# One tile is normed, scored and routed beside the output product, and the slabs behind it are paced by four slots

## The reference, cut to what matters

```python
h = h + einsum('btc,cd->btd', mixed, w_out)                # the output product
xb = rmsnorm(h, ffn_norm_w)                                # for each block of 128 tokens:
q = einsum('nd,dc->nc', xb, w_query).reshape(128, 8, 2, 128)
s = einsum('nhpc,hpkc->nhpk', q, subkeys)                  # 8 heads, 2 halves, 128 keys
sv, si = top_k(s, 16)
cand_s = sv[:, :, 0, :, None] + sv[:, :, 1, None, :]       # 16 x 16 candidates
cand_i = si[:, :, 0, :, None] * 128 + si[:, :, 1, None, :]
top_s, pos = top_k(cand_s.flat, 16)                        # 16 experts of a head
experts, gates = cand_i[pos], softmax(top_s)               # 128 experts of a token
hid = gelu(einsum('nkd,nd->nk', u_table[experts], xb)) * gates
y = einsum('nk,nkd->nd', hid, v_table[experts])
```

## Time and profile before

| what | value |
|---|---|
| median of 3 runs | 2848.63 us (2845.56 to 2849.38) |
| profiled execution, its own time | 2850.17 us |
| its span, first to last instruction | 2848.4 us |
| its mean granted TensorE clock | 0.978 |
| PE, DVE, ACT, POOL busy | 91%, 65%, 45%, 25% of the span |
| HBM read | 746.77 MB, 263 GB/s over the span |

### The profile page before, as it was taken

One profiled execution on the slowest core, in us unless ns is written; L12 is line 12 of the kernel. 1 busy time (PEld: TensorE's weight loads), 2 busy tenths in 40 slices (PEclk: granted clock), 3 DMA queues, 4 the chain that ended last, 5 costly groups with the idle time before them and its releaser, 6 DMA issues. The chain is left out here.

```text
span 2848.4 us, 32530 instructions
## 1 busy us (share of the span) xinstructions
PE 2594.6 (91%) x11450; PEld 1789.5 (63%) x11450; DVE 1840.9 (65%) x3807; ACT 1282.7 (45%) x2860; POOL 707.6 (25%) x661
## 2 busy tenths in 40 slices
PE   8998969989799977799989999899999898999998
PEld 8886755434355523255555555399788577788887
DVE  7787467777777767777777776655564774433323
ACT  3244234454454445556556555445325564232222
POOL 3210014444344434444444434200000110000000
PEclk9999989999899999999999999999999999999999
DMA  7853049999999999999999999766332103132322
GB/s 286 280 162 122 16 184 406 421 410 407 394 420 420 416 415 418 416 413 419 419 412 410 417 415 415 289 193 209 106 96 58 39 24 111 45 103 90 104 96 74
DMA packets 133843, 751.11 MB, mean 264 GB/s; under 512 B 19504, under 2 KB 20048, under 8 KB 67472
## 3 DMA queue, kind: packets, MB, share of 16 engines
q0 software_dynamic: 82320, 575.94, 50.0%
q1 hardware_dynamic: 51072, 173.02, 17.4%
q10 hardware_dynamic: 288, 0.07, 0.0%
HBM read 746.77 MB, written 2.10 MB: 263 GB/s over the span
## 5 line engine op out<-in xcount | busy, mean ns | idle before, releaser
L1848 PE MATMUL peer_y<-rows,diag 128*128 128x512 f32 x2048 | 996.3, 613 | 152.4 <-ACT diag L1828 141.0
L1802 DVE CUSTOM_DVE_ANT_0 rows<-rows,hidden 128x1024 f32<-128x1024 f32 x512 | 627.4, 1225 | 353.0 <-DMA rows<-in_peer_table,experts 350.7
L1789 POOL DMA_INDIRECT rows<-in_peer_table,experts x512 | 608.0, 1187 | 952.3 <-PE peer_y L1848 793.4
L1848 PEld LDWEIGHTS peer_y<-rows,diag 128*128 128x128 f32 x2048 | 364.0, 192 | 549.7 <-issue 293.2
L1825 ACT ACTIVATE hid<-hid 128x1 f32<-128x1 f32 x512 | 102.6, 200 | 530.0 <-DVE hid L1802 526.4
L2462 DVE TENSOR_TENSOR piece_w_low<-piece_raw,piece_w_high 128x1024 fp32r<-128x1024 f32 x132 | 161.4, 1223 | 96.7 <-ACT piece_w_high L2457 96.5
L1828 ACT ACTIVATE diag<-ident,hid 128x128 f32<-128x128 f32 x512 | 205.6, 401 | 16.6
L2457 ACT ACTIVATE piece_w_high<-piece_raw 128x1024 fp32r<-128x1024 f32 x132 | 138.8, 1052 | 105.0 <-PE out_bank L161 77.6
L1826 ACT ACTIVATE hid<-hid,gates 128x1 f32<-128x1 f32 x512 | 150.8, 295 | 16.6
L159 PE MATMUL peer_y<-peer_feat_high,early_w_high 128*128 128x256 f32 x352 | 144.5, 410 | 1.8 <-issue 1.8
L426 ACT ACTIVATE proj_w_high<-proj_raw 128x1024 fp32r<-128x1024 f32 (+2 forms) x57 | 57.6, 1013 | 189.5 <-PE proj_pair L161 98.9
(11 more groups left out here) (624 smaller groups left out, 5541.5 us busy)
## 6 DMA issues: line engine op xcount, KB each, us to landing
ada<-in_w_ada POOLq DMA_DIRECT2D x96, 384.0 KB, 4.6
piece_raw<-in_ffn_w_gate SPq DMA_DIRECT2D x44, 512.0 KB, 3.5
piece_raw<-in_ffn_w_up SPq DMA_DIRECT2D x44, 512.0 KB, 4.4
piece_raw<-in_ffn_w_down SPq DMA_DIRECT2D x44, 512.0 KB, 3.5
query_raw<-in_peer_w_query SPq DMA_DIRECT2D x32, 512.0 KB, 7.9
early_raw<-in_ffn_w_gate SPq DMA_DIRECT2D x22, 512.0 KB, 8.2
early_raw<-in_ffn_w_up SPq DMA_DIRECT2D x22, 512.0 KB, 8.0
early_raw<-in_ffn_w_down SPq DMA_DIRECT2D x22, 512.0 KB, 7.8
```

The source lines that it names most:

```text
L1789: pool.indirect_dma_start(self.rows[:, b, :], None, self.table, bass.IndirectOffsetOnAxis(ap=self.experts[:, unit % self.SETS, n % TOPK:n ...
L1802: dve.tensor_tensor_reduce(out=self.rows[:, b, 0:D], in0=self.rows[:, b, 0:D], in1=self.hidden[:, tile, :], scale=1.0, scalar=0.0, op0=ALU ...
L1848: last = pe.matmul(self.y[self.bank(tile)][:, c * BANK:(c + 1) * BANK], self.diag[:, b, :], self.rows[:, b, D + c * BANK:D + (c + 1) * BAN ...
```

## The change

Tile 0 is normed alone, as soon as its two units of the output product are added, in the first half of unit 2 of the product. Its features, two slabs of queries with 128 columns only (`first_query`), their scores (against keys loaded beforehand in a small tile of their own) and 14 routing steps of unit 0 run in the block of the output product, before unit 3's sum is added and tile 1 is normed. POOL gathers slots 0 to 3 in that block, and slots 4 and 5 when tile 1's features are done, since the scratch tiles of the norm now lie in those two buffers. The slabs' first two are split earlier. The 24 `column` products of units 0 to 3 all stand in units 0 and 1. In `peer_scores` slabs 0 and 1 are asked for tile 1 only; AHEAD is 4 and PACE 4 in the first half, so that slabs 4 to 15 have slots beside them, and END is 56, not 58. The load of all keys moves from the end of the output product to the head of that block. Behind the first six dots no routing step is done, behind the next 16 two, then one. The exponentials of a unit are done on ACT ahead of the slot's work at other slots than before (`exps_before`).

```diff
...
+    FREE_ROWS, ROUTED = 4, 14
...
-        behind = Scratch(nc, t.meta_at + 4 * D, None)
-        tile_sq = behind.sbuf("peer_sq", [P, 2, D])
+        last_rows = experts.last_rows(FREE_ROWS)
+        tile_sq = last_rows.sbuf("peer_sq", [P, D])
         tile_ss = spare.sbuf("peer_ss", [P, 2])
-        diag = behind.sbuf("peer_diag", [P, 2, P])
-        full = behind.sbuf("peer_full", [P, 2, 2, W2])
+        diag = last_rows.sbuf("peer_diag", [P, 2, P])
+        full = last_rows.sbuf("peer_full", [P, 2, 4, P])
+        first_keys = last_rows.sbuf("first_keys", [P, 2, NK])
...
+        peer_bank = [l_bank[1], l_bank[2]]
+        first_q = [l_bank[3][:, 0, :], l_bank[1][:, 0, :]]
+        first_s = l_bank[2][:, 0:2, :]
...
-            sp.wait_ge(out_done, 4)
-            sp.dma_start(keys[:, :, :], dram["peer_subkeys"]).then_inc(keys_in.handle, 16)
+            sp.wait_ge(o_summed, TT)
+            sp.dma_start(first_keys[:, :, :], dram["peer_subkeys"][:, 0:2, :]).then_inc(keys_in.handle, 16)
+            experts.load(sp, dram)
...
+            experts.gathers_to(pool, FREE_ROWS)
+            pool.wait_ge(low, 4)
+            experts.gathers_to(pool, experts.RING)
...
             weights.high_first(act)
...
+            def tile_root(i):
+                act.wait_ge(x_added, 2 * i + 2)
+                act.activation(tile_sq[:, :], t.x[:, i, :], ACT.Square, accum_out=tile_ss[:, i:i + 1]).then_inc(tile_summed, 1)
+                act.wait_ge(tile_ms, i + 1)
+                act.activation(tile_ss[:, i:i + 1], tile_ss[:, i:i + 1], ACT.Sqrt).then_inc(tile_rstd, 1)
+            def tile_high(i):
+                for g in range(2):
+                    act.wait_ge(whole, 2 * i + g + 1)
+                    act.activation(feat_parts.high[:, 4 * g:4 * g + 4, i * P:(i + 1) * P], full[:, g, :, :], ACT.Copy)\
+                       .then_inc(high, 1)
+            tile_root(0)
+            tile_high(0)
+            for b in range(2):
+                act.wait_ge(weights.used.handle, weights.used.at(b + 1))
+                act.activation(query[:, b, 0:P], first_q[b], ACT.Copy).then_inc(first_moved, 1)
+            act.wait_ge(tile_rstd, 1)
+            tile_root(1)
+            tile_high(1)
+            experts.exponentials(act, 0)
...
-            for u in range(4):
+            dve.wait_ge(turned, 4)
+            weights.low_first(dve)
+            def add_rows(u):
                 tile, c = u // 2, u % 2
                 dve.wait_ge(out_done, u + 1)
                 x = t.x[:, tile, c * BANK:(c + 1) * BANK]
                 dve.tensor_tensor(x, x, turn_bank[u], ALU.add).then_inc(x_added, 1)
...
+            def tile_scale(i):
+                own = tile_ss[:, i:i + 1]
+                dve.wait_ge(tile_summed, i + 1)
+                chain.link(dve.tensor_scalar(own, own, 1.0 / D, EPS, ALU.mult, ALU.add))
+                dve.reciprocal(own, own).then_inc(tile_ms, 1)
+                dve.wait_ge(tile_rstd, i + 1)
+                dve.tensor_scalar(diag[:, i, :], t.ident[:, :], own, None, ALU.mult).then_inc(diag_ready, 1)
+            def tile_parts(i):
+                for g in range(2):
+                    dve.wait_ge(bank_turned, 2 * i + g + 1)
+                    if i:
+                        dve.wait_ge(low, g + 1)
+                    for f in range(4 * g, 4 * g + 4):
+                        last = dve.tensor_scalar(full[:, g, f % 4, :], peer_bank[g][:, f % 4, :], t.ffn_norm[:, f:f + 1], None,
+                                                 ALU.mult)
+                    last.then_inc(whole, 1)
+                for g in range(2):
+                    own = (slice(0, P), slice(4 * g, 4 * g + 4), slice(i * P, (i + 1) * P))
+                    dve.wait_ge(high, 2 * i + g + 1)
+                    dve.tensor_tensor(feat_parts.low[own], full[:, g, :, :], feat_parts.high[own].bitcast(F32), ALU.subtract)\
+                       .then_inc(low, 1)
+            def tile_hidden(i):
+                dve.scalar_tensor_tensor(hidden[:, i, :], t.x[:, i, :], tile_ss[:, i:i + 1], row_w[:, :], ALU.mult, ALU.mult)
+            add_rows(0)
+            add_rows(1)
+            tile_scale(0)
+            add_rows(2)
+            tile_parts(0)
             dve.wait_ge(row_in, 16)
-            for i in range(2):
-                dve.scalar_tensor_tensor(hidden[:, i, :], t.x[:, i, :], tile_ss[:, i:i + 1], row_w[:, :], ALU.mult, ALU.mult)
-            weights.low_first(dve)
-            for g in range(5):
-                if g < 4:
-                    dve.wait_ge(bank_turned, g + 1)
-                    if g >= 2:
-                        dve.wait_ge(low, g - 1)
-                    for f in (2 * g, 2 * g + 1):
-                        last = dve.tensor_scalar(full[:, g % 2, f % 2, :], peer_bank[g][:, f % 2, :], t.ffn_norm[:, f:f + 1],
-                                                 None, ALU.mult)
-                    last.then_inc(whole, 1)
-                if g >= 1:
-                    two = slice(2 * g - 2, 2 * g)
-                    dve.wait_ge(high, g)
-                    dve.tensor_tensor(feat_parts.low[:, two, :], full[:, (g - 1) % 2, :, :],
-                                      feat_parts.high[:, two, :].bitcast(F32), ALU.subtract).then_inc(low, 1)
+            tile_hidden(0)
+            dve.wait_ge(first_scored, 2)
+            chain.link(dve.tensor_copy(scores[:, 0:2, :], first_s))
+            experts.route(dve, ROUTED)
+            add_rows(3)
+            tile_scale(1)
+            tile_parts(1)
+            tile_hidden(1)
...
-            for u in range(4):
+            def out_rows(u, chunks):
                 i, c = u // 2, u % 2
-                for f in range(KC):
+                for f in chunks:
                     last = pe.matmul(turn_bank[u], feat[:, f, i * P:(i + 1) * P], w_out[:, c, f, :],
                                      start=(f == 0), stop=(f == KC - 1))
-                    if f % 4 < 3:
-                        column(24 + 6 * u + f // 4 * 3 + f % 4)
-                last.then_inc(out_done, 1)
-            pe.wait_ge(diag_ready, 1)
-            for g in range(4):
-                for f in (2 * g, 2 * g + 1):
-                    for i in range(2):
-                        last = pe.matmul(peer_bank[g][:, f % 2, i * P:(i + 1) * P], t.x[:, i, f * P:(f + 1) * P], diag[:, i, :],
-                                         start=True, stop=True)
-                last.then_inc(bank_turned, 1)
+                    if u < 2 and f % 4 < 3:
+                        for n in range(2):
+                            column(24 + 12 * u + f // 4 * 6 + f % 4 * 2 + n)
+                    if f == KC - 1:
+                        last.then_inc(out_done, 1)
+            def turn_tile(i):
+                pe.wait_ge(diag_ready, i + 1)
+                for f in range(KC):
+                    last = pe.matmul(peer_bank[f // 4][:, f % 4, :], t.x[:, i, f * P:(f + 1) * P], diag[:, i, :], start=True,
+                                     stop=True)
+                    if f % 4 == 3:
+                        last.then_inc(bank_turned, 1)
+            def first_query(b):
+                pe.wait_ge(weights.low.handle, weights.low.at(b + 1))
+                for k in range(KC):
+                    last = product(pe, first_q[b], weights.columns(b, slice(k * P, (k + 1) * P)),
+                                   (feat_parts.high[:, k, 0:P], feat_parts.low[:, k, 0:P]), start=(k == 0), stop=(k == KC - 1))
+                last.then_inc(weights.used.handle, 1)
+            def first_score(b):
+                pe.wait_ge(first_moved, b + 1)
+                pe.matmul(first_s[:, b, :], query[:, b, 0:P], first_keys[:, b, :], start=True, stop=True)\
+                    .then_inc(first_scored, 1)
+            out_rows(0, range(KC))
+            out_rows(1, range(KC))
+            out_rows(2, range(4))
+            turn_tile(0)
+            out_rows(2, range(4, KC))
+            pe.wait_ge(low, 2)
+            first_query(0)
+            first_query(1)
+            out_rows(3, range(1))
+            pe.wait_ge(keys_in.handle, keys_in.at(16))
+            first_score(0)
+            first_score(1)
+            out_rows(3, range(1, KC))
+            turn_tile(1)
...
+    QB, RING, PACE = 2 * PH, weights.RING, 5 if half else 4
+    AHEAD = 0 if half else 4
...
+        def tiles_of(b):
+            return range(int(half == 0 and b < 2), 2)
+        def columns_of(b):
+            return slice(tiles_of(b).start * P, W)
...
-                experts.load(sp, dram)
+                sp.dma_start(keys[:, :, :], dram["peer_subkeys"]).then_inc(keys_in.handle, 16)
...
+                own = columns_of(b)
...
-                if half == 0 and b == max(ROUTE) + 1:
-                    experts.exponentials(act, 0)
...
-                if half == 0 and b in ROUTE:
-                    if b == min(ROUTE):
-                        dve.wait_ge(s_moved.handle, s_moved.at(2))
-                    experts.route(dve, ROUTE[b])
...
+    STEPS, BEHIND = TOPK, 6
```

(49 more changed lines are left out.)

28 lines of the change are left out of this document (9 added, 19 removed).

## The result

| | before | after |
|---|---|---|
| median | 2849.06 us (5 runs, 2845.56 to 2850.09) | 2864.38 us (5 runs, 2862.28 to 2866.68) |
| profiled span | 2848.4 us | 2863.1 us |
| granted clock, mean of the span | 0.978 | 0.976 |

The account below looks back on a forecast made before the run. Bytes bound the gather stretch, so the start of continuous transfer sets the end. Full flow 4.6 us later, less 0.2 for fewer bytes, gave +4.4 on the median 2848.63: 2853.0 us, range 2844 to 2864.

Parts of the forecast that it names:

- Part 2: Tile 0's features after unit 2 of the output product: PE waits uncovered from 359.6 to 364.5, 4.9 us.
- Part 3: Tile 0's two 128-column slabs: 5.4 us for the first, 2.9 for the second; routing begins at 374.5.
- Part 4: Routing and first gathers: first gather asked at 383.7, 16.6 us earlier than before; next block starts at 395.2.
- Part 5: Block of scores to first dot: slab 2 lands 8.6 us in, first dot at 414.9, 2 us later than before.
- the 81 ns quoted in Part 3: Skill's figure for a 128-column load and product: a slab would be 1.9 us, the total some 3 us better; not adopted.
- The sum itself: Slot 0 free at 422.6, full flow at 424.6: 4.6 us later, less 0.2 for 0.1 MB, makes +4.4 us.
- rival (c): Gather stretch from 460 on runs at 418 GB/s, not 414, as requests come steadier: net -8.6, 2840 us; chance 0.11.
- (b): DVE or PE becomes the bound in the 48 slots, a slab taking 12.0 instead of 11.4 us: 2860 us; chance 0.08.
- Rival (a): Half-wide products in slabs 0 and 1 of both tiles cost like f32 ones: +13.6 in all, 2862 us; chance 0.21.
- Rival (d): High clock throughout and slab 2 landing as if alone: net -2.2, 2846.4 us; chance 0.10.

Follow-up runs that it names:

- e2: Changed kernel with slabs 2 and 3 and the full keys asked in the earlier block, that of the output product; 2858.87 us, ratio 1.0036.
- e4: Changed kernel with no gather in the block of the output product, the ring of six asked in the block of scores; 2863.71 us, ratio 1.0058.
- e1: Changed kernel with all eight chunks of unit 3 of the output product ahead of tile 0's two half-wide slabs; 2861.85 us, ratio 1.0045.
- e3: e2 with slabs 0 and 1 of the block of scores multiplied for both tiles, 256 columns; 2853.35 us, ratio 1.0019.
- e7: Kernel before with only the new pace (AHEAD 4, PACE 4, END 56, routing steps and exponentials moved), merge block as before; 2847.54 us, ratio 0.9996.
- e12: Kernel before with the new pace of e7 and the early split of e8, merge block untouched; 2842.60 us, ratio 0.9978.
- e5: Changed kernel with the edits of e1, e2 and e3 together, full keys asked when the first scores are made; 2849.99 us, ratio 1.0000.
- e6: Changed kernel with the old pace again in the block of scores (AHEAD 6, PACE 5); 2864.50 us, ratio 1.0051.
- e11: e5 with slots 0 to 3 dotted ahead of slab 2's split and multiplied in slab 1, 4 and 5 in slab 3; 2851.21 us, ratio 1.0003.
- e8: Kernel before with only the splits of the first two slabs moved ahead of the units' sums; 2848.66 us, ratio 0.9995.
- e10: Changed kernel with only slabs 0 and 1 of the block of scores made 256 columns wide; 2862.73 us, ratio 1.0041.

## Why the prediction missed

By its own steps, predicted against measured:

| step | predicted | measured | off by |
|---|---|---|---|
| Part 2, slabs start | 364.5 | 366.21 | +1.7 |
| Part 3, routing starts | 374.5 | 379.88 | +5.4, of it 3.7 new |
| Part 4, first gather | 383.7 | 389.07 | +5.4, none new |
| Part 4, next block starts | 395.2 | 400.28 | +5.1, none new |
| Part 5, slab 2 landed behind that | 8.6 | 13.1 | +4.5 |
| Part 5, landing to first dot | 11.1 | 14.2 | +3.1 |
| first dot | 414.9 | 427.59 | +12.7 |
| slot 0 free, seventh gather | 422.6 | 434.90 | +12.3 |

**The step of Part 5 that failed** is the landing of slab 2: "With 2.7 us of the last two gathers still to move, slab 2 lands 4.6 + 1.3 + 2.7 = 8.6 us into the block". It took the first four gathers for nearly gone. Six gathers, the keys and slabs 2 and 3 are 8.4 MB; at 414 GB/s that is 20.3 us from 391, two microseconds behind the first gather, so it ends at 411.4, 11.1 us into the block, and ScalarE had the data 2.0 later. The transfer engines were full to 412 and then nearly empty. My own numbers allowed this sum: the distance from first gather to block was right (11.5 against 11.2), the bytes between were not counted. In that step's own terms, the keys landed at 10.1 us (I had 4.6 + 2.7) and slab 2 3.0 behind them (I had 1.3). e2 takes the wait away and gets 5.7 us back; without gathers ahead (e4) slab 2 lands at 8.9.

**The second is the clock in Part 3 and Part 5.** I priced the first half-wide slab at the low clock (5.4) and the second at the full one (2.9), as the full-wide slabs do. The price at each clock was right: e1 shows 0.11 us a product at 1.00 and after shows 0.21 at 0.50; the 81 ns quoted in Part 3 appear in no run. But the clock did not rise. Stretches of the changed kernel:

```profile
368.00:372.00 4.00, 4.00 (x20) 4.00 (x20) 0.00 (x0) 0.28 (x1) 0.00 (x0) 0.50 0.00 0
372.00:376.00 4.00, 4.00 (x21) 4.00 (x21) 0.00 (x0) 0.00 (x0) 0.00 (x0) 0.50 0.00 0
...
404.00:408.00 4.00, 4.00 (x21) 4.00 (x20) 0.00 (x0) 0.28 (x1) 0.00 (x0) 0.50 0.98 373
```

That cost 2.0 us in the slabs of Part 3 (10.3 against 8.3), 1.7 in the chunk, the scores and the copy behind them (3.4 against 1.7), and in the next block it left slab 2 at 1.2 GHz, 5.5 us in place of 2.9. e3 against e2 prices it: 5 us.

**What held.** The sum itself: with the measured seventh gather in its place it gives 434.90 + 2.0 - 420 - 0.2 = 16.7 us, against the 16 measured. So the mechanism was right, and the landing of slab 2 and the slabs' clock were too small in it. Routing to first gather is 9.2 us as counted, the way from the end of routing to the next block 11.5 against 11.8, first dot to seventh gather 7.3 against 7.7. The gather stretch is unchanged (414 GB/s, share 1.01), so rival (c) falls and so does (b), by e7. Rival (a) as written (half-wide products at the price of f32) falls by e1, yet its time, 2862, was nearest: the price was doubled by the clock, not by the type. Rival (d) took the good side of both costs, and both went to the bad one. Part 2's +1.7 is in part the profile's own offset (the output product starts 1.3 later than before).

**What the change is worth in parts.** Its pace and early split gain 6.3 us without its merge block (e12). So tile 0 alone in the block of the output product costs some 22 us: 1.0056 less 0.9978 is 0.78%. With e1, e2 and e3 on top (e5) it still costs 6 us. (The runs were made on different chips, each beside runs of the kernel before.) What it buys, gathers asked 9 to 16 us sooner, is worth nothing net by e4: six buffers fill and then wait for slab 3, and in after they also hold back the keys and slab 2. The MB column puts the kernels nearly in the order of their times, and 414 GB/s turns it into microseconds within about 4 (after: 6.8 MB, 16 us); e4, e6, e11 and e12 show that the rest of the span moves by some microseconds between profiles.

**Open:** the rate of 412 against 414 and 415 GB/s in e11; why e6's later first dot cost nothing; what early gathers are worth when they delay no load; whether e7 and e8 add up or one of them carries e12. No version with slots early and routing of unit 1 early was made.

## What to carry to other kernels

Moving the start of a transfer stream forward gains only if its buffers are emptied sooner too: follow the first buffer to its release, and count every byte asked ahead of the load that this release needs. Work that is split in halves to start sooner can run at half the speed: look at the granted clock of the stretch, not at the product's shape. And judge a stream's start by bytes moved at a fixed time, not by one event in it.

## What the runs showed of the hardware that I had not expected

- An fp32r product of 128 columns takes 0.213 us at a granted 0.50 and 0.111 at 1.00; one of 256 columns takes the same 0.213 at 0.50 (e5, 393.37 to 397.85) and 0.12 at 1.00. Half the columns save nothing at the low clock and 7% at the full one.
- PE, busy in full or nearly so with 128-column products, stayed at 1.2 GHz for the whole of two such stretches (366.2 to 376.5 and 400.3 to 408.8 in after; e1 shows the second again, 395.8 to 404.3), while 256-column products brought 2.4 GHz in the place of the second (e3, e5, e10). Coming in at 2.4 GHz, 5.7 us of 128-column products kept it (e1: 1.00 from 368 to 372, 0.99 to 376). The Trainium skill, "TensorE: Matmul & The Clock Gate", section "Part 1: The HAM clock gate", ties the clock to how busy the engine has lately been; these two stretches don't agree, since PE was busy in full in them and stayed at 0.50.
